# Layer 1's mixer: other places for the steps of the triangular inverses, a chunk's weights and some clears and fills

## The reference

```
p = h @ w_in
z, xbc, dt_raw, rw = split_cols(p, (SSM_INNER, SSM_CONV_W, SSM_HEADS, RW_IN))
xbc = silu(causal_conv(xbc, ssm_conv_w, ssm_conv_b))          # 4 taps
y   = ssd_chunked(xh, dt, A, B, C)                            # chunks of 128 tokens
y   = group_rmsnorm((y + ssm_d * xh) * silu(z), ssm_norm)
rw  = rw + (token_shift(rw) - rw) * rw_mu                     # r, k, v and three low-rank inputs
step: sa = S kk;  S = S * w - sa b' + v k';  y = S r          # rwkv7, token by token
y_rw = (head_layernorm(yr) * ln_w + ln_b + bonus) * g
out = concat(y_ssm, y_rw) @ w_out
```

## Time and profile before

| | us |
|---|---|
| median of 3 runs | 1278.99 |
| lowest and highest | 1278.82, 1284.99 |
| the profiled execution | 1280.63 |
| its span, first to last instruction | 1278.8 |
| PE busy in it | 1243.7 (97%) |
| DVE, ACT, POOL busy | 736.2, 614.8, 587.8 |
| mean granted TensorE clock | 0.991 of full |

### The profile page before, as it was taken

The page is one execution under the profiler, slowest core; times in us unless marked ns, Lnnn a source line. Parts: engine busy times, 40 slices in busy tenths (PEclk is TensorE's granted clock), DMA queues, the critical chain, the costliest instruction groups (busy, mean ns, idle before and its releaser), DMA issues.

```text
span 1278.8 us, 19294 instructions
## 1 busy us (share of the span) xinstructions
PE 1243.7 (97%) x7550; PEld 1055.7 (83%) x7550; DVE 736.2 (58%) x1102; ACT 614.8 (48%) x991; POOL 587.8 (46%) x685
## 2 busy tenths in 40 slices
PE   7999989999999999999999999999999999999997
PEld 5877757888988989987788778888888898998986
DVE  3528676562743725644899956477564372662743
ACT  5345665461552724635662625743454272461641
POOL 5653214765074262654364533321756426265080
PEclk9999999999999999999998989999999999999999
DMA  8332102335251451332222321000334344152311
GB/s 277 92 83 66 51 17 67 101 113 149 67 163 36 131 133 50 97 86 60 57 68 65 85 65 50 2 2 17 95 103 123 92 132 132 52 145 68 99 34 66
DMA packets 173258, 108.40 MB, mean 85 GB/s; under 512 B 4590, under 2 KB 170736, under 8 KB 173168
## 3 DMA queue, kind: packets, MB, share of 16 engines
q1 hardware_dynamic: 172688, 107.09, 29.5%
q0 software_dynamic: 480, 0.08, 0.0%
HBM read 105.05 MB, written 2.10 MB: 84 GB/s over the span
## 4 chain that ended last, share of the span: by engine, by line
PE 86%; DVE 9%; ACT 3%; issue 2%; DMA 0%; DVEq 0%; SPq 0%; ACTq 0%
PE ps L1256 9%; PE ps L1255 9%; PE ps L1257 9%; PE ps L1221 6%; PE ps L1220 6%; PE ps L1219 6%; PE ps L1124 6%; PE ps L1126 5%; PE ps L1125 5%; PE ps L1111 2%; PE ps L1235 2%; PE ps L1234 2%; PE ps L1233 2%; PE ps L1604 1%; DVE arena L2860 1%
## 5 line engine op out<-in xcount | busy, mean ns | idle before, releaser
L1014 POOL TENSOR_TENSOR w_lo<-raw_w,w_hi 128x256 fp32r<-128x256 f32 x248 | 213.4, 891 | 276.8 <-ACT w_hi L1760 276.8
L2485 DVE TENSOR_TENSOR h<-h,ps 128x512 f32<-128x512 f32 x64 | 44.0, 687 | 207.2 <-PE ps L1257 207.2
L1124 PE MATMUL ps<-hn_hi,w_hi 128*128 128x512 f32 x368 | 153.0, 416 | 1.4 <-DVEq L2576 1.0
L1126 PE MATMUL ps<-hn_hi,w_lo 128*128 128x512 f32 x368 | 145.5, 395 | 0.0
L1125 PE MATMUL ps<-hn_lo,w_hi 128*128 128x512 f32 x368 | 145.2, 395 | 0.0
L1070 POOL TENSOR_TENSOR wx_lo<-raw_w,wx_hi 128x256 fp32r<-128x256 f32 x128 | 97.9, 796 | 40.1 <-ACT wx_hi L1827 40.1
L1827 ACT ACTIVATE wx_hi<-raw_w 128x1024 fp32r<-128x1024 f32 x62 | 65.4, 1054 | 104.0 <-PE ps L1257 91.5
L1070 POOL TENSOR_TENSOR wx_lo<-y_mix,wx_hi 128x256 fp32r<-128x256 f32 x64 | 51.6, 837 | 135.8 <-ACT wx_hi L1827 135.8
L1827 ACT ACTIVATE w_hi<-raw_w 128x1024 fp32r<-128x1024 f32 x54 | 57.0, 1055 | 110.7 <-PE ps L1257 100.5
L1070 POOL TENSOR_TENSOR w_lo<-raw_w,w_hi 128x256 fp32r<-128x256 f32 x120 | 89.9, 780 | 40.1 <-ACT w_hi L1827 40.1
L1256 PE MATMUL ps<-hid_lo,w_hi 128*128 128x512 f32 x256 | 100.7, 394 | 0.0
(11 more groups left out here) (484 smaller groups left out, 3327.9 us busy)
## 6 DMA issues: line engine op xcount, KB each, us to landing
raw_w<-in_w_up SPq DMA_DIRECT2D x40, 512.0 KB, 4.2
raw_w<-in_w_down SPq DMA_DIRECT2D x40, 512.0 KB, 4.1
raw_w<-in_o_w_in SPq DMA_DIRECT2D x27, 512.0 KB, 3.8
y_mix<-in_w_up SPq DMA_DIRECT2D x24, 512.0 KB, 4.5
y_mix<-in_w_down SPq DMA_DIRECT2D x24, 512.0 KB, 4.5
raw_w<-in_e_w_in SPq DMA_DIRECT2D x19, 512.0 KB, 3.9
raw_w<-in_e_w_out SPq DMA_DIRECT2D x8, 512.0 KB, 3.5
raw_w<-in_o_w_out SPq DMA_DIRECT2D x8, 512.0 KB, 3.7
```

The costliest lines, as they stand in the source:

```text
L1014: nc.gpsimd.tensor_tensor(w_lo[:, n % CUT, ks], raw_w[:, n % RING, ks], w_hi[:, n % CUT, ks].bitcast(F32), ALU.subtract).then_inc(w_cut, 1)
L1124: mm(o, a_hi, b_hi, start=(k == 0), stop=False)
L1126: ins = mm(o, a_lo, b_hi, start=False, stop=(k == KT - 1))
```

## The change

- DVE: in the slots of the convolutions (i=10 to 16) only steps 0 to 3 of `substitute` stay; steps 4 to 26 are put between the pieces of the chunks up to `ssd_back(1)`/`ssd_front(2)`, the rest and the transposes behind those. `ssd_weights(1)` goes ahead of `take_staged(17)`. `ssd_back` is cut into `ssd_scaled`, `ssd_added` and `ssd_summed`; for chunk 3 the first goes ahead of `take_staged(21)` and the last behind `masked(0, 0)`.
- ACT: `fill_columns(0)` goes from slot 24 to behind the decays of slot 25, `fill_columns(1)` from behind the draining of `g_tok` into `high_merge(0)`.
- POOL: the clear of `inv_t[0]` goes from slot 24 to slot 26, that of `inv_dp` from behind `low_part` of the output projection's second unit to ahead of it.

```
# POOL
+                    if n == base["out", 1] + CUT - 1:
+                        full(pool, "rw", 11)
+                        nc.gpsimd.memset(inv_dp, 0.0).then_inc(S["inv_zero"], 1)
                     pool.wait_ge(w_high, n + 1)
                     low_part(n)
-                    if n == base["in", 1] + 24:
+                    if n == base["in", 1] + 26:
                         pool.wait_ge(S["inv_ready"], 1)
                         nc.gpsimd.memset(inv_t[0], 0.0).then_inc(S["inv_zero"], 1)
                     if n == base["out", 1] + CUT - 1:
-                        full(pool, "rw", 11)
-                        nc.gpsimd.memset(inv_dp, 0.0).then_inc(S["inv_zero"], 1)
                         pool.wait_ge(S["mixed"], 14)
# ACT
-                if j == 24:
-                    fill_columns(0)
                 if j in (19, 21, 23, 25):
                     ssd_decays((j - 19) // 2)
+                if j == 25:
+                    fill_columns(0)
...
                 if n == 0:
+                    fill_columns(1)
                     act.wait_ge(S["z_silu"], NT)
...
                 drain(g_tok[:, t, :], "g_tok", t)
-            fill_columns(1)
# DVE
-            take_staged(10)
-            substitute(0, 2)
-            conv_staged(10)
-            substitute(2, 4)
-            take_staged(11)
-            substitute(4, 6)
-            conv_staged(11)
-            substitute(6, 8)
-            for i in range(12, 17):
+            for i in range(10, 17):
                 take_staged(i)
-                substitute(2 * i - 16, 2 * i - 15)
+                if i >= 13:
+                    substitute(i - 13, i - 12)
                 conv_staged(i)
-                substitute(2 * i - 15, 2 * i - 14)
...
-            substitute(18, 20)
+            substitute(4, 8)
             ssd_front(0)
-            substitute(20, 22)
+            substitute(8, 12)
             ssd_weights(0)
-            substitute(22, 31)
+            substitute(12, 20)
+            ssd_back(0)
+            ssd_front(1)
+            substitute(20, 22)
+            ssd_weights(1)
+            take_staged(17)
+            substitute(22, 24)
+            shift(17)
+            substitute(24, 26)
+            take_staged(18)
+            substitute(26, 27)
+            shift(18)
+            ssd_back(1)
+            ssd_front(2)
+            substitute(27, 31)
             V.transpose(inv_rows, sub_inv.rearrange("p t c -> p c t"))
             link(V.transpose(inv_cols, sub_inv))
             dve.sem_inc(S["inv_ready"], 1)
-            take_staged(17)
-            ssd_back(0)
-            shift(17)
-            ssd_front(1)
-            take_staged(18)
-            ssd_weights(1)
-            shift(18)
-            ssd_back(1)
-            ssd_front(2)
+            ssd_weights(2)
             take_staged(19)
-            ssd_weights(2)
             shift(19)
             take_staged(20)
             shift(20)
             ssd_back(2)
             ssd_front(3)
             ssd_weights(3)
+            ssd_scaled(3)
             take_staged(21)
             shift(21)
-            ssd_back(3)
+            ssd_added(3)
...
             masked(0, 0)
+            ssd_summed(3)
             keep_pairs(0)
```

More of the change, by code:

```diff
@@ L3018, in ssd_weights, with ssd_scaled @@
                 ins.then_inc(free_sem("cb", n), 1)
-            def ssd_back(n):
+            def ssd_scaled(n):
                 y = xs_tok[:, n, :]
@@ L3024, in ssd_back, with ssd_added @@
                 link(V.tensor_tensor(h8(y), h8(y), over(row("ssm_d", 8), 2, 64), ALU.mult))
+            def ssd_added(n):
+                y = xs_tok[:, n, :]
                 o = full(dve, "y_diag", n)
@@ L3032, in ssd_back, with ssd_summed @@
                     drained(dve, "y_off", n)
-                    link(V.tensor_tensor(y, y, y_tmp, ALU.add))
+            def ssd_summed(n):
+                y = xs_tok[:, n, :]
+                link(V.tensor_tensor(y, y, y_tmp, ALU.add))
+            def ssd_back(n):
+                ssd_scaled(n)
+                ssd_added(n)
+                if n:
+                    ssd_summed(n)
                 if n < NT - 1:
@@ L3043, in ssd_back @@
                     dve.sem_inc(S["s_new"], 1)
-            substitute(18, 20)
+            substitute(4, 8)
             ssd_front(0)
-            substitute(20, 22)
-            ssd_weights(0)
-            substitute(22, 31)
+            substitute(8, 12)
+            ssd_weights(0)
+            substitute(12, 20)
+            ssd_back(0)
+            ssd_front(1)
+            substitute(20, 22)
+            ssd_weights(1)
[9 more added lines that the diff above has]
+            substitute(27, 31)
             V.transpose(inv_rows, sub_inv.rearrange("p t c -> p c t"))
```

## The result

The changed kernel takes 1268.07 us (median of 4 runs, 1267.37 to 1268.96), the kernel before in the same series 1278.98. The ratio of the runs is 0.9893, 95% interval 0.9874 to 0.9911, which is 13.7 us less (11.4 to 16.1) and sets the time at 1265.3; by the medians it is 10.9 us, between the profiled executions 1280.63 - 1268.96 = 11.7, between their spans 1278.8 - 1266.9 = 11.9. The mixer is faster, by more than the 9.3 us forecast, and by the ratio just beyond the range's lower end of 1265.8; the median of its own runs, 1268.07, lies inside the range.

The account below looks back on a forecast made before the run. PE bounds the kernel, busy 1243.7 of 1278.8 us. 3.0 + 5.5 - 2.0 + 0.8 + 1.6 = 8.9, with 0.4 of offsets 9.3 us: 1271.3 for the profiled execution, median 1269.7, range 1265.8 to 1274.0.

Parts of the forecast that it names:

- Steps out of the convolution slots: Waits ahead of `x_tok` (1.6), for low parts (0.4) and ahead of `ssd_front(0)` (1.0) go: 3.0 us gained.
- 0.7 unrecorded: Small offsets beside the recorded waits, 9.2 us early with them against 8.5 without; half, 0.4 us, counted.
- The wait ahead of `ssd_back(1)`: Earlier `ssd_weights(1)` removes PE's wait of 2.13 us and the low clock behind it, 3.4 us: 5.5 us gained.
- What is late next: DVE late after `take_staged(18)`: new waits of 0.9 us ahead of `ssd_back(2)` and 1.1 ahead of `ssd_back(3)`, -2.0 us.
- The rival without a new wait: POOL and DVE miss each other, chain behind `take_staged(18)` under 16 us: 12.4 us gained, 1266.6 us; chance 0.25.
- The tail of chunk 3: Cutting `ssd_back(3)` shortens the wait of 1.63 us ahead of `p_low`; with DVE in arrears 0.8 us gained.
- `fill_columns(1)`: Moved to where ACT waits for z, it drains `rhs` earlier and ends the wait ahead of `u`: 1.6 us gained.
- POOL's clears, `fill_columns(0)`: Moving POOL's clears and ACT's fill was worth nothing, bounds -0.5 and 0.3 us.
- DVE beside POOL: By the port rule one-input transposes aren't slowed: 3.2 us for the two, wait ahead of `ssd_back(2)` 0.5 instead of 0.9.

Follow-up runs that it names:

- a5: Kernel after with 18 steps of the inverses back in the convolution slots, in place of 4; ratio to before 0.9927.
- b1: Kernel before with only `fill_columns(1)` of ACT moved; ratio to before 0.9964 over 10 runs.
- b2: Kernel before with only `ssd_weights(1)` put ahead of `take_staged(18)`, still behind `take_staged(17)`; ratio to before 0.9984.
- a2: Kernel after with `ssd_weights(1)` back behind `take_staged(18)`; span 1270.6 us, ratio to before 0.9931.
- a1: Kernel after with ACT's `fill_columns(1)` back behind the draining of `g_tok`; span 1268.9 us, ratio to before 0.9922.
- a4: Kernel after with `ssd_back(3)` in one piece behind `shift(21)`; span 1266.8 us, ratio to before 0.9915.
- a3: Kernel after with POOL's clear of `inv_t[0]` back at slot 24; ratio to before 0.9940.
- f1: Kernel after with `ssd_weights(2)` ahead of the last steps and transposes, and `shift(20)` later; median 1269.58 us, ratio to before 0.9897.
- c1: Kernel after with PE's bonus products in four parts behind slots 13 to 16; bonus to `x_tok` took 30.1 us, 1.2 more.
- d1: Kernel after with the bonus products in four parts and `take_staged(10)` ahead of DVE's last block copies; median 1265.69 us, ratio to before 0.9875.

## Why the prediction was too cautious

- **Steps out of the convolution slots**: forecast 3.0 us and 0.7 unrecorded, of which the sum took half; measured 31.61 - 28.90 = 2.7 and 27.6 - 26.6 = 1.0, 3.7. Right in mechanism, DVE's last convolution within 0.2 us of its place, a5 confirms it. 0.3 us too low, and partly luck: bonus to `x_tok` took 27.3 to 28.9 us in executions that are the same up to there, so the 2.7 could have been 4.3. With the steps in the slots it took 31.3 to 31.6 whatever the clock did, since where the bonus products ran faster (b1, b2, a5) PE waited 1.3 to 1.5 us for low parts ahead of slot 16. Of such waits the prediction had the 0.4 that the profile of before shows.
- **The wait ahead of `ssd_back(1)`**: forecast 2.13 and 3.4 for the clock; measured 2.3 and, between `(1)` and `(2)`, 20.3 to 16.9 without the new wait, 3.4. The weights were done at 739.1, forecast between 738.5 and 740.5. Right for this execution. What was wrong is that I took 3.4 us as the price of such a wait: with waits of 2.1 and 2.6 us b1 and a2 paid 1.8. Nor did the end of slot 23 hold the weights, as I had it, but that of slot 22 (b2).
- **What is late next**: here the prediction failed. It named the two new waits and their places, but gave them 2.0 us, and left 0.8 of the wait ahead of `p_low`. Measured are 0.39 and 0.32 us in the list, 0.56 and 0.59 by the stretches, and nothing at `p_low`, where the whole 1.6 us came in. Together 1.65 of the 2.2 us that are missing in the sum. I had DVE in arrears at `take_staged(18)`, starting at 748.0, and 16.9 us for the chain behind it. It started at 747.27, on time, because three of the four instructions after `shift(17)` ran at the pace of an idle POOL (0.32 to 0.34 us, one 0.87), and took 16.6 to the end of the weights at 763.9; in a1 and a4 it took 16.1, and PE did not wait ahead of `ssd_back(2)` at all. So what I carried on as 1 us of arrears was at most half of that: the second wait was 0.6 and not 1.1, and `masked` ended at 781.5, ahead of `p_low` at 781.83. The terms that I listed for the chain also add up to 14.5 and 17.9 us, not to 13.9 and 17.4. The rival without a new wait, 12.4 us at a chance of 0.25, came nearer to the 11.5 than the 9.3.
- **The tail of chunk 3** and **`fill_columns(1)`**: 1.59 and 1.67 us, forecast 0.8 and 1.6. a4 shows that cutting `ssd_back(3)` carries 1.1 of the first, a1 that ACT and not the named releaser held `u`. For the first, the 0.8 that I left standing is the same fault as above: DVE was not 1 us late.
- **POOL's clears, `fill_columns(0)`**: rightly at nothing; a3 shows what hung on that of `inv_t[0]`. The clear of `inv_dp` and `fill_columns(0)` were not put back by themselves, so that they are worth nothing is not shown.
- **DVE beside POOL**: the steps, with two inputs, take 0.42 us (256 columns) while POOL is idle and 0.93 (255 columns) beside it. The transposes, with one input, took 2.11 and 1.22 us though POOL's low part lay beside both (759.31 to 762.15), near the 2.00 and 1.20 of before. The Trainium skill (SBUF — State Buffer, section "SBUF: two separate sides") has the rule: whichever of the two starts first holds the shared ports against the other for its whole instruction, an instruction of DVE with two SBUF inputs only against one of GpSimd that reads SBUF. These rows agree with it. By it I had 3.2 us for the transposes and a wait of 0.5 us ahead of `ssd_back(2)`; measured 3.3 and 0.4 to 0.6. I should have taken that for the transposes; that the wait came out as well is partly luck, since in other executions it is nothing.

The sum is 9.3 against 11.5 us over the stretch. The 2.2 us that are missing are 1.65 of waits forecast and not met, 0.3 at the steps and 0.2 at `ssd_back(1)`. The distance from 11.5 to the ratio's 13.7 is in no trace. The means of the times listed, 1280.44 and 1268.12 us, are 12.3 apart, with one of the four before, 1284.99, 6 us above the others; where the rest comes from is open.

## What to carry to other kernels

In a kernel that one engine fills to 97%, count its waits, then ask for each what holds it; the view's releaser can be wrong, and undoing one edit on the chip tells. When work moves out of one gap, write down the next deadline of the engine that takes it, as a sum from its last real wait on. Behind a wait of 1 to 3 us TensorE paid between 0 and 3.4 us more here by its clock, and not the same in each run, so single spans can't judge an edit of 1 us; the same stretch in several traces can, if the traces that lack the edit are looked at too: f1's first 0.6 us was there without it.

## What the runs showed of the hardware that I had not expected

The granted clock falls behind short waits in some executions and not in others. The wait of 2.13 us cost 3.4 us more, one of 2.14 (b1) 1.8, one of 2.64 (a2) 1.8, one of 1.54 (b2) 0.1; the same 0.99 us ahead of `ssd_front(0)`, behind another of 1.6 us, cost nothing in before and 1.6 to 1.8 us in b2 and a5; the same 1.63 us at `p_low` nothing in before and 1.6 in b1. Where it cost something the clock fell to 0.50, the level of 1.2 GHz, within 2.3 us of the work's beginning again; in a3 and c1, with waits of 4.49 and 2.83 us, just before it began. 4.8 us of products of 2 columns bring it down as well, without any wait: the products and slot 14 behind them took 10.7 to 12.3 us in kernels that are the same up to there (the products 3.7 to 4.7 of it). In parts of 0.95 us, with nothing waiting, they left it at 1.00 (d1). When a two-input step and POOL's low part start within 0.02 us of each other, the step took 0.29 us in seven executions and 0.86 in two, and that decided a wait of PE.
